# Norms with an early root on ScalarE, other counts of added squares on VectorE, and zero matmuls in the waits of TensorE

## What is computed

```python
def rmsnorm(x, g):
    xf = x.astype(jnp.float32)
    y = xf * lax.rsqrt(jnp.mean(xf * xf, axis=-1, keepdims=True) + RMS_EPS)
    return (y * g.astype(jnp.float32)).astype(x.dtype)
...
    h = rmsnorm(x, g) * (1.0 + scale[:, None, :]) + shift[:, None, :]
...
def swiglu(h, w_gate, w_up, w_down):
    return (jax.nn.silu(h @ w_gate) * (h @ w_up)) @ w_down
```

## Time and profile before

| | |
|---|---|
| median of 3 runs | 2075.44 us (2074.5 to 2076.27) |
| the profiled execution, in all | 2077.19 us |
| its span, first to last instruction | 2075.4 us |
| mean granted TensorE clock | 0.953 |
| TensorE matmul busy | 1911.9 us (92%) |
| VectorE busy | 1254.2 us (60%) |
| ScalarE busy | 763.4 us (37%) |
| transfers | 370.96 MB, mean 179 GB/s |
| roots of L942; table loads on that line | 13; 11 |

### The profile page before, as it was taken

One profiled execution on the slowest core, in us unless ns is written; L12 is line 12 of the kernel. 1 busy time (PEld: TensorE's weight loads), 2 busy tenths in 40 slices (PEclk: granted clock), 3 DMA queues, 4 the chain that ended last, 5 costly groups with the idle time before them and its releaser, 6 DMA issues.

```text
span 2075.4 us, 34471 instructions
## 1 busy us (share of the span) xinstructions
PE 1911.9 (92%) x13735; PEld 1792.8 (86%) x13740; DVE 1254.2 (60%) x1924; ACT 763.4 (37%) x1114; POOL 125.5 (6%) x176
## 2 busy tenths in 40 slices
PE   2999999989999999998999998837999999699999
PEld 2999888867899999998879998736999989579998
DVE  6566655674466666758645444894766613547665
ACT  3344311031333354435444434323444411354442
POOL 0000000100000000000110000540000000130000
PEclk9999999999999999999999998967999999699999
DMA  9677644911377747766624553311455424114552
GB/s 394 230 285 269 236 160 144 377 46 61 132 259 277 263 145 284 269 249 226 246 82 167 188 187 126 122 41 61 162 183 182 162 102 145 39 43 152 188 185 81
DMA packets 51051, 370.96 MB, mean 179 GB/s; under 512 B 5664, under 2 KB 5664, under 8 KB 6048
## 3 DMA queue, kind: packets, MB, share of 16 engines
q1 hardware_dynamic: 41760, 302.81, 40.4%
q0 software_dynamic: 9216, 67.11, 8.3%
HBM read 368.86 MB, written 1.05 MB: 178 GB/s over the span
## 4 chain that ended last, share of the span: by engine, by line
PE 83%; DVE 11%; ACT 3%; issue 1%; DMA 1%; POOL 0%; DVEq 0%; SPq 0%; ACTq 0%; POOLq 0%
PE up L486 12%; PE up L485 12%; PE up L487 12%; PE up L478 11%; PE acc L487 6%; PE acc L486 6%; PE acc L485 6%; DVE arena L1629 4%; PE acc L543 3%; PE up L746 3%; PE acc L654 2%; DMA mring<-in_mods 1%; DVE w_lo L1242 1%; PE stat L457 1%; PE stat L463 1%
## 5 line engine op out<-in xcount | busy, mean ns | idle before, releaser
L1242 DVE TENSOR_TENSOR w_lo<-ring,w_hi 128x2048 fp32r<-128x2048 f32 x198 | 453.5, 2291 | 266.0 <-ACT w_hi L984 265.9
L485 PE MATMUL up<-H_hi,w_hi 128*128 128x256 f32 x2112 | 595.8, 282 | 9.2 <-DVE w_lo L1242 9.0
L486 PE MATMUL up<-H_lo,w_hi 128*128 128x256 f32 x2112 | 597.6, 283 | 0.0
L487 PE MATMUL up<-H_hi,w_lo 128*128 128x256 f32 x2112 | 593.2, 281 | 0.0
L984 ACT ACTIVATE w_hi<-ring 128x2048 fp32r<-128x2048 f32 x198 | 377.9, 1909 | 232.6 <-PE acc L487 123.0
L485 PEld LDWEIGHTS up<-H_hi,w_hi 128*128 128x128 f32 x2112 | 400.2, 190 | 14.5 <-DVE w_lo L1242 9.9
L487 PEld LDWEIGHTS up<-H_hi,w_lo 128*128 128x128 f32 x2112 | 401.2, 190 | 0.0
L486 PEld LDWEIGHTS up<-H_lo,w_hi 128*128 128x128 f32 x2112 | 399.2, 189 | 0.0
L478 PE MATMUL up<-H,ring 128*128 128x256 f32 x1280 | 287.8, 388 | 15.8 <-DVE arena L1604 14.5
L486 PE MATMUL acc<-hid_lo,w_hi 128*128 128x256 f32 x1056 | 298.8, 283 | 0.0
L487 PE MATMUL acc<-hid_hi,w_lo 128*128 128x256 f32 x1056 | 298.8, 283 | 0.0
(11 more groups left out here) (245 smaller groups left out, 2116.0 us busy)
## 6 DMA issues: line engine op xcount, KB each, us to landing
ring<-in_weights SPq DMA_DIRECT2D x276, 1024.0 KB, 4.8
mring<-in_mods POOLq DMA_DIRECT2D x64, 1024.0 KB, 7.6
mring<-in_mods SPq DMA_DIRECT2D x8, 1024.0 KB, 10.1
con<-in_constants SPq DMA_DIRECT2D x1, 1408.0 KB, 16.3
X<-in_x SPq DMA_DIRECT2D x1, 1024.0 KB, 13.4
out<-X SPq DMA_DIRECT2D x1, 1024.0 KB, 3.9
cact<-in_c SPq DMA_DIRECT2D x1, 512.0 KB, 3.4
vec<-in_vectors SPq DMA_DIRECT2D x1, 467.0 KB, 4.1
```

What stands on the lines that cost most here:

```text
L485: mm(dst, hi, x_hi, start=start, stop=False, skip_group_check=True)
L486: mm(dst, hi, x_lo, start=False, stop=False, skip_group_check=True)
L487: return mm(dst, lo, x_hi, start=False, stop=stop, skip_group_check=True)
L1242: dve.tensor_tensor(w_lo[s % 3][:, :], ring[:, n % RING, :], w_hi[s % 3][:, :].bitcast(F32), ALU.subtract).then_inc(split_ready, 1)
```

## The change

ScalarE's program for a norm begins with a root of `eps` (128 x 1) into a scratch column `spare`. VectorE adds two squares instead of three behind a feed-forward (1 and 2), and five instead of three behind slots (1, 2, and 3 to 5 in one go behind update 5); where neither is behind (the conformer's two norms) three stay. TensorE sums the tiles that are left: six behind a feed-forward, three behind slots. The four matmuls that clear `acc` move from the start of the feed-forward to the place between the last sum and the wait for the reciprocal. In the norms ahead of other layers four matmuls of zeros into the second bank of `up` stand there instead (`idle(4)`), and in all norms with added squares five more (`idle(5)`) follow the spread. Ahead of them TensorE waits until the banks of `up` are free (`pair_free`), also in the norm inside the ssm, which gets no zero matmuls. The first norm has no added squares and gets only the moved clearing.

```diff
@@ -161,6 +161,7 @@
         eps = sb("eps", [P, 1])
+        spare = sb("spare", [P, 1])
@@ -354,6 +355,7 @@
         PRE = 4
+        PRE_OF = {"ffn": 3, "slots": 6}
@@ -441,7 +443,12 @@
-            def sum_tiles(src, n, presum=True, done=0):
+            def idle(n):
+
+                for _ in range(n):
+                    mm(up[:, 1, :], zeros[:, 0:P], zeros[:, :], start=True, stop=True, skip_group_check=True)
+
+            def sum_tiles(src, n, presum=True, done=0, pre=PRE, zero=False):
...
-                    if presum and 1 <= m < PRE:
+                    if presum and 1 <= m < pre:
                         continue
...
                 ins.then_inc(stat_ready, 1)
+                for b in range(4 if zero else 0):
+                    mm(acc[:, b, :], zeros[:, 0:P], zeros[:, :], start=True, stop=True, skip_group_check=True)
+                pe.wait_ge(pair_free, state["free"])
+                if presum and not zero:
+                    idle(4)
                 state["rcp"] += 1
                 pe.wait_ge(rcp_ready, state["rcp"])
                 for tt in range(2):
                     ins = mm(stat[:, L + tt * P:L + (tt + 1) * P], rtok[:, tt:tt + 1].to_broadcast([P, P]), ident,
                              start=(tt == 0), stop=True, skip_group_check=True)
                 ins.then_inc(spread_ready, 1)
-
-            def norm(presum=True):
-                sum_tiles(H, KD, presum)
+                if presum:
+                    idle(5)
+
+            def norm(presum=True, zero=False, behind=None):
+                sum_tiles(H, KD, presum, pre=PRE_OF.get(behind, PRE), zero=zero)
@@ -488,8 +502,6 @@
             def ffn():
                 f0, s0 = state["free"], state["split"]
-                for b in range(4):
-                    mm(acc[:, b, :], zeros[:, 0:P], zeros[:, :], start=True, stop=True, skip_group_check=True)
@@ -907,27 +919,27 @@
-            norm(presum=False)
+            norm(presum=False, zero=True)
             ffn()
-            norm()
+            norm(behind="ffn")
             ssm(AT_SLOT["ssm"])
-            norm()
+            norm(zero=True, behind="slots")
             ffn()
-            norm()
+            norm(zero=True, behind="ffn")
             ffn()
-            norm()
+            norm(behind="ffn")
             moba(AT_SLOT["moba"])
-            norm()
+            norm(zero=True, behind="slots")
             ffn()
-            norm()
+            norm(behind="ffn")
             state["h"] += KD
             norm()
             conformer(AT_SLOT["conf"])
-            norm()
+            norm(zero=True, behind="slots")
             ffn()
-            norm()
+            norm(behind="ffn")
             nsa(AT_SLOT["nsa"])
-            norm()
+            norm(zero=True, behind="slots")
             ffn()
@@ -943,6 +955,7 @@
             def norm(scale, shift=None, mod=False, dest=H, own=False, first=False, parts=False, hi=H_hi):
+                act.activation(spare[:, :], eps[:, 0:1], ACT.Sqrt)
                 for m in range(KD):
@@ -1263,13 +1276,13 @@
-            def add_square(m):
+            def add_square(m, pre=PRE):
...
-                if m == PRE - 1:
+                if m == pre - 1:
                     ins.then_inc(presum_ready, 1)
                     state["sq"] += KD
@@ -1360,8 +1373,8 @@
                     update(m, how)
-                    if m >= 2 and square:
-                        add_square(m - 2)
+                    if m in (3, 4) and square:
+                        add_square(m - 2, PRE_OF["ffn"])
@@ -1369,8 +1382,8 @@
                     update(m, how)
-                    if m >= 2:
-                        add_square(m - 2)
+                    for k in {3: (1,), 4: (2,), 5: (3, 4, 5)}.get(m, ()):
+                        add_square(k, PRE_OF["slots"])
                     if m in (3, 5):
                         low(n0 + KD // per, (m - 3) // 2)
```

More of the change, by code:

```diff
@@ L1264, in fold @@
                 ins.then_inc(mod_used, 1)
-            def add_square(m):
-                if not 1 <= m < PRE:
+            def add_square(m, pre=PRE):
+                if not 1 <= m < pre:
                     return
```

## The result

The changed kernel takes 2083.9 us as the median of 6 runs (2081.72 to 2086.99), the kernel before 2075.7 us (2074.5 to 2078.13) on the same chip: a ratio of 1.004, 95% interval [1.0027, 1.0053]. That is 8.2 us slower, and the interval leaves out no change. The profiled execution of the changed kernel is the fastest of its six, 2081.72 us with a span of 2079.9, and that of the kernel before, 2077.19 us, is slower than its median: so the two traces show 4.5 us (2079.9 less 2075.4) of the 8.2. Runs of the changed kernel spread over 5.3 us, those of before over 3.6. Of the experiments' executions, one of `h_order_nofill` (5329.16 us) and one of `j_ffn_as_before` (4197.56 us) lie far outside and are left out of the comparisons; they move no median by more than 0.02 us.

What follows compares the result with a forecast made beforehand. It took the short gaps at the norms to count, with a chain of ScalarE and VectorE waits behind slots. Terms 3.8 + 1.0 - 1.2 + 3.6 - 0.7 + 2.0 + 7.9 + 1.5 - 9.6 = +8.3 gave 2083.8 us, range 2074 to 2090.

Steps and rivals of the forecast that it cites:

- The table load: Slot norms: three early loads of 1.28 us on the chain, +3.8; early roots there and after the final norm, +1.0.
- The saving ahead of the real root: Norms: removing the load there gives only what it ended later than TensorE's sums, -1.2 us.
- The additions: Behind slots: two more VectorE additions ahead of the second remainder, which gates updates 6 and 7, 4 x 0.9 = +3.6 us.
- Longer waits: Slot norms: TensorE waits longer for square 6, so the last eight sums fall to half clock, +2.0 us.
- Fillers ahead of the root: Between sums and root wait in eleven norms: four zero matmuls delay the spread, +7.9 us (bounds 1 and 9.5).
- Fillers behind the spread and the returning clock: Before layers' first matmuls: five fillers delay, +1.5 us; full clock returns sooner after norms, -9.6 (bounds 0 and -12.8).
- The sum of all fillers: All norms with fillers: delays ahead of root +7.9 and behind spread +1.5, against the clock's -9.6 us.
- Rival A: From sums to first matmul: fillers keep TensorE at 2.4 GHz through the norms; -8.8, 2066.6 us; chance 0.08.
- Rival B: Slot chain has slack, TensorE releasing update 6, so its costs fall away; -1.9, about 2073.5 us; chance 0.05.
- C: In the norms, fillers mostly run at full clock: cost 3 instead of 9.4, clock -11; +0.5, 2075.9 us; chance 0.15.
- D: After norms, clock returns no sooner than the matmuls bring it: -4 instead of -9.6; +13.9, 2089.3 us; chance 0.17.

Runs made afterwards that it cites:

- h_order_nofill: Changed kernel with, behind slots, the early root ahead of both roundings and both remainders ahead of five additions, without any fillers: 2066.82 us, 0.9952 of the kernel before.
- j_ffn_as_before: g_slots_all with norms behind feed-forwards as in the kernel before (no early root in the norm, three added squares): 2056.25 us, 0.9911 of the kernel before.
- ab_both: Changed kernel without the early root behind slots and with three added squares there instead of five: 2072.74 us, 0.9981 of the kernel before.
- a_no_load: Changed kernel without the early root on spare in the four norms behind slots: 2079.62 us, 1.0017 of the kernel before.
- f_ahead_only: Changed kernel with fillers ahead of the root only, none behind the spread: 2096.47 us, 1.0108 of the kernel before.
- c_no_fill: Changed kernel without idle(4) and idle(5), the clearing of acc back behind the spread: 2086.28 us, 1.005 of the kernel before.
- d_fill_only: Kernel before with only the fillers and the moved clearing added: 2074.79 us, 0.9994 of the kernel before.
- g_slots_all: Changed kernel with, behind slots, the early root ahead of both roundings and both remainders ahead of five additions, all fillers kept: 2054.43 us, 0.9907 of the kernel before.
- b_adds3: Changed kernel with three added squares behind slots instead of five: 2078.24 us, 1.0012 of the kernel before.

## Why the prediction was right, point by point

**Direction and size.** Forecast 2083.8 us, +8.3; measured 2083.9 and +8.2. The mechanism of the loss is the one forecast, as `ab_both` shows. For the chain behind slots the terms come to 3.84 + 0.8 - 0.95 + 3.6 + 2.0 = 9.3 us (0.95 is the part of the 1.2 that falls to conformer and nsa), and without fillers the four gaps grow by 9.6 in the traces (32.2 to 41.8). That the whole came within 0.1 us is partly luck. In the traces the forecast is too high by 3.8 us (+8.3 against +4.5), mostly because fillers cost less in the gaps than was put down; the medians show the 8.2, and where their other 3.7 us lie no trace shows.

**The table load**, +3.8 and +1.0 less 1.2: the load stands where it was put, 1.28 us, with a root of 0.20 where 0.2 was taken. Taking it away gave 4.5 us for an expected 4.6. The saving ahead of the real root was overrated: the sums at half clock took the place of the load. In `a_no_load`, where the load is back in that place, it ends 0.29 us before the last norm's sums. It would have cost nothing there, so nothing was saved. On the Trainium skill's drain of 1.38 us ("ScalarE: Activation LUTs", "What ACT_TABLE_LOAD costs"): here the chain has 0.02 us between the load's end (1870.18 + 1.28) and the root at 1871.48, and the load starts 0.01 us behind the rounding's end (1870.17); these runs don't show one.

**The additions**, +3.6: each is 0.45 us, 0.9 per norm in the traces; the run without them gave 5.9 by the medians and 4.1 in the gaps behind slots, together with what follows from the longer wait.

**Longer waits**, +2.0: the sums take 1.87 us in the last norm, as forecast, against 1.22 before. The two costs undone one at a time shorten the gaps behind slots by 4.4 and 4.1 us, together by 11.3; the 2.8 us between 8.5 and 11.3 are what only the undoing of both gives back, and this term is the forecast's part of that kind.

**Fillers ahead of the root**, +7.9 with 9.5 as upper bound. Alone they cost 8.1 us in the traces (`f_ahead_only` against `c_no_fill`), all in the gaps, as the term said; by the medians it is 10.2 to 11.7, and the 2 to 4 us beyond are not located. The price of the last norm was right (its spread starts at 1883.88, 1.52 us behind the sums' end at 1882.36; 1.6 was named). Where they end in a gap they bring no clock back: the rest is 1981.6 us in both traces.

**Fillers behind the spread and the returning clock**, +1.5 - 9.6 = -8.1. Too small: -13.8 us between the changed kernel and `f_ahead_only`, -12.7 in the traces. There the layers give -10.5, close to the -9.6, and the gaps shrink by 2.2 where +1.5 was put down. Behind the first feed-forward the clock came back during the fillers (0.61 in the window 242.00 to 244.60) and the layer's first 3.8 us ran at 1.00, where the earlier trace rows had 4.1 us at 0.50. One place was missed: in nsa, TensorE's 7.0 us shrank to 4.25, near the 3.8 that were named, but VectorE's clearing and tables, hidden until then, became what TensorE waits for, and the matmuls after it ran at half clock for 5 us.

**The sum of all fillers** was put at -0.2 and is -2.1 (`c_no_fill`) or -1.2 (`d_fill_only`), neither clear of noise. In the traces of the changed kernel and `c_no_fill` it is 5.9 - 10.5 = -4.6, where the terms said 9.4 - 9.6: the gain was sized well, the cost too high.

**Rival A** is what happens with a shorter wait: the clock held in every slot norm of `g_slots_all`. In the changed kernel it doesn't. The reason given against A was half right: in the last norm the clock falls before the fillers, but in the wait for square 6 and not in the sums. The Trainium skill's advice against idle gaps ("TensorE: Matmul & The Clock Gate", "Why this matters for your kernels") agrees with these traces in direction: before the last eight sums of that norm TensorE idles 2.38 us and the clock falls, in `g_slots_all` it idles 0.63 and the clock holds. Fillers ahead of a gap don't help; they cost 8.1 us in the traces and 10.2 to 11.7 by the medians.

**Rival B** has fallen with `a_no_load` and `b_adds3`: nothing in the slot chain had slack. **C** (2075.9 us) and **D** (2089.3) lie on both sides of the measured time. In the traces the fillers' balance, -4.6, lies midway between the forecast's -0.2 and C's -8. D's clock term fell: the layers are 10.5 us shorter than without fillers (8.5 against the kernel before), not 4.

What stays open: why single runs of the changed kernel differ by 5 us, and with it the 3.7 us between the medians and the traces. The clock falls at slightly different places of the same work from kernel to kernel (behind the first feed-forward 0.50 in the window 239.20 to 242.00 of `f_ahead_only`, 0.75 in the changed kernel's); that it also does so from run to run is only argued, since each kernel has one trace.

## What to carry to other kernels

Moving a fixed cost out of one wait is worth nothing if the order of the same engine's queue puts it ahead of what another engine waits for; read from the chain which instruction stands in front before choosing the place. Here the same early root and the same additions lost 8 us in one place and, ahead of the roundings and behind the remainders, were part of a kernel 20 us faster than the one before (ratio 0.9907). Matmuls of zeros paid here only where they reached up to the next layer's work; ahead of a wait they were a cost. Shorten the wait first, which took 11.9 us by itself in the traces, then fill what is left.

## What the runs showed of the hardware that was not expected

Fillers are not additive. By the medians, against none: ahead of the root alone +11.7 us, behind the spread alone -2.0, both -2.1, and both with the shorter wait -11.1. In the layers alone, by the traces, they give 0.0, -7.2, -10.5 and -11.9. The same eight sum instructions of one column cost 1.05 us at a granted clock of 1.00 and 1.87 at 0.50, so a longer wait ahead of them lengthens the chain twice.
